# One convolved piece made a step earlier, and its successor's load issued a step earlier, in the RG-LRU recurrence of a hybrid mixer layer

## What is computed

```python
xc = dwconv(vx, conv_w, conv_b, 2, 1)          # latent; cc likewise of the context
for d, rev in enumerate((False, True)):        # forward and backward
    a_c, b_c = lru_coeffs(cc, ...)             # r, i = sigmoid(xc @ wa), sigmoid(xc @ wx) per head of 64
    h_c = linear_scan(a_c, b_c, None, rev)     # h_t = a_t h_prev + b_t
    h0 = h_c[:, 0] if rev else h_c[:, -1]
    a_x, b_x = lru_coeffs(xc, ...)             # a = exp(-8 r softplus(-lam)); b = sqrt(1 - a^2) * (i * xc)
    y_x = y_x + linear_scan(a_x, b_x, h0, rev)
```

## Time and profile before

| | us |
|---|---|
| median of 3 runs (lowest, highest) | 797.6 (796.71, 797.98) |
| the profiled execution, in all | 795.27 |
| its span | 793.2 |
| TensorE busy | 740.0 (93%) |
| VectorE busy | 534.0 (67%) |
| ScalarE busy | 449.4 (57%) |
| GpSimd busy | 273.5 (34%) |

### The profile page before, as it was taken

The page is one execution under the profiler, slowest core; times in us unless marked ns, Lnnn a source line. Parts: engine busy times, 40 slices in busy tenths (PEclk is TensorE's granted clock), DMA queues, the critical chain, the costliest instruction groups (busy, mean ns, idle before and its releaser), DMA issues.

```text
span 793.2 us, 9934 instructions
## 1 busy us (share of the span) xinstructions
PE 740.0 (93%) x3468; PEld 602.5 (76%) x3468; DVE 534.0 (67%) x811; ACT 449.4 (57%) x743; POOL 273.5 (34%) x321
## 2 busy tenths in 40 slices
PE   3876989999999998999998999989999999999997
PEld 1575767888888877888887887758787888888885
DVE  4377654759997789788996655776645665766532
ACT  4266652798786975887984982334535133534311
POOL 0022335243435254224433456223211145443421
PEclk9596999999999998999999999989999999999999
DMA  9998003334355245344453134344458667967531
GB/s 363 347 324 242 27 28 107 93 97 117 116 181 173 64 157 173 99 126 137 163 167 112 58 104 142 98 146 147 115 197 305 224 209 252 307 214 264 180 114 76
DMA packets 89218, 130.11 MB, mean 164 GB/s; under 512 B 22768, under 2 KB 54128, under 8 KB 87632
## 3 DMA queue, kind: packets, MB, share of 16 engines
q1 hardware_dynamic: 84800, 115.44, 45.0%
q0 software_dynamic: 4368, 14.03, 6.4%
HBM read 91.17 MB, written 38.27 MB: 163 GB/s over the span
## 4 chain that ended last, share of the span: by engine, by line
PE 72%; DVE 8%; issue 6%; DMA 5%; ACT 5%; POOL 3%; SPq 1%; DVEq 0%; ACTq 0%; POOLq 0%
PE bank L1543 23%; PE bank L1545 23%; PE bank L1544 23%; DMA wm<-in_w_mod 3%; DVE xg L1186 1%; ACT bank L878 1%; ACT fbuf L895 1%; POOL xTh L609 1%; DVE xTl L1194 1%; DMA pv<-scratch_u 1%; PE bank L1579 1%; DVE xg L1166 1%; DMA wraw<-in_w_in 1%; PE bank L1669 1%; PE bank L1559 0%
## 5 line engine op out<-in xcount | busy, mean ns | idle before, releaser
L1543 PE MATMUL bank<-xTh,wh 128*128 128x512 f32 (+1 forms) x592 | 237.0, 400 | 7.4 <-DVE xTl L1194 4.0
L1545 PE MATMUL bank<-xTh,wl 128*128 128x512 f32 (+1 forms) x592 | 231.3, 391 | 0.0
L1544 PE MATMUL bank<-xTl,wh 128*128 128x512 f32 x576 | 226.9, 394 | 0.0
L1543 PEld LDWEIGHTS bank<-xTh,wh 128*128 128x128 f32 x592 | 112.8, 190 | 32.9 <-DVE xTl L1194 5.7
L1545 PEld LDWEIGHTS bank<-xTh,wl 128*128 128x128 f32 x592 | 112.5, 190 | 23.5
L1544 PEld LDWEIGHTS bank<-xTl,wh 128*128 128x128 f32 x576 | 109.8, 191 | 22.5 <-issue 1.2
L1543 PE MATMUL bank<-xTh 128*128 128x512 f32 (+1 forms) x272 | 104.2, 383 | 1.9 <-issue 1.4
L1544 PE MATMUL bank<-xTl,xTh 128*128 128x512 f32 x256 | 99.6, 389 | 0.0
L1545 PE MATMUL bank<-xTh,xTl 128*128 128x512 f32 x256 | 99.6, 389 | 0.0
L911 ACT ACTIVATE ustage<-bank 128x512 f32<-128x512 f32 x56 | 33.0, 593 | 92.3 <-PE bank L1545 75.9
L609 POOL TENSOR_SCALAR sph<-xc 128x512 fp32r<-128x512 f32 (+1 forms) x36 | 26.9, 762 | 122.1 <-PE bank L1545 67.5
(11 more groups left out here) (192 smaller groups left out, 1428.8 us busy)
## 6 DMA issues: line engine op xcount, KB each, us to landing
scratch_u<-ustage SPq DMA_DIRECT2D x72, 256.0 KB, 3.2
wraw<-in_w_in SPq DMA_DIRECT2D x18, 512.0 KB, 5.2
wm<-in_w_mod SPq DMA_DIRECT2D x8, 1024.0 KB, 14.4
xg<-in_x SPq DMA_DIRECT2D x16, 512.0 KB, 9.2
yb<-scratch_y SPq DMA_DIRECT2D x32, 256.0 KB, 3.6
gb<-scratch_u SPq DMA_DIRECT2D x32, 256.0 KB, 5.0
xres<-in_x SPq DMA_DIRECT2D x16, 512.0 KB, 4.7
out<-tout SPq DMA_DIRECT2D x15, 512.0 KB, 3.0
```

The source lines that it names most:

```text
L1543: mm(out, wh_, xh_, start=first, stop=False)
L1544: mm(out, wh_, xl_, start=False, stop=False)
L1545: return mm(out, wl_, xh_, start=False, stop=last)
```

## The change

On GpSimd, `load_v(after + 2)` is issued in step s = NCH - 1 = 3 (the fourth step of a tile) instead of in the last one, s = 4. On VectorE, `conv(after + 1)` leaves the head of the last step, where it stood behind `gate_w_lo(t + 1)`, and stands at the end of the fourth step, behind its scans, its weight parts and its `gate_sum`, if it has one. Both happen for t = 0, 1 and 2.

```diff
@@ GpSimd's loop
                 if s == 2 and more:
                     load_gate_w(t + 1)
                     load_v(after + 1)
-                if s == NCH and more:
+                if s == NCH - 1 and more:
                     load_v(after + 2)
                 gated_input(q)
@@ VectorE's loop
                 if s == NCH and t + 1 < N_LRU:
                     gate_w_lo(t + 1)
-                    conv(after + 1)
                 for j in convs_in_step(q, 4):
                     conv_glu(j)
                 one_minus_a2(q)
...
                 if s == 2 and t + 1 < N_LRU:
                     conv(after)
+                if s == NCH - 1 and t + 1 < N_LRU:
+                    conv(after + 1)
                 if s == NCH and t + 1 < N_LRU:
                     conv(after + 2)
```

## The result

The changed kernel is faster: 790.66 us (median, 786.94 to 793.11) against 796.61 us (792.53 to 797.98) for the kernel before, measured beside it, a ratio of 0.9925 with a 95% interval of 0.9908 to 0.9943. That is 6.0 us, where 2.8 were forecast. The time lies 0.5 us under the low end of the range. Of the 4.1 us between 794.8 and 790.66, 1.0 is the kernel before itself, which the prediction took at 797.6; the rest is the saving. Faster was right in sign; the sum was less than half of what came.

The account below looks back on a forecast made before the run. TensorE was taken to bound the kernel, with step 9's stall a wait for VectorE's cvzl. Stall 1.8 plus clock 0.95, about 2.8 us saved, other terms 0, gave 794.8 us; range 791.2 to 797.4.

Parts of the forecast that it names:

- R1: Rival, step 9: whole stall goes, as cvz gets in ahead of Ib or holds are rarer; saves 6.4, 791.2 us; chance 0.13.
- the sign for "right": Step 9: TensorE's idle time before the conv unit would be 2 to 3 us if the forecast held.
- The kept part from Qb to the restart: Step 9: from Qb's start to TensorE's restart it takes 3.18 us, unchanged by the edit.
- the size of the stall: Step 9: moving the conv shrinks TensorE's stall by 1.8 us, from 4.33 to about 2.5.
- one gwh of 0.42 slips between: Step 9: a GpSimd gwh of 0.42 us delays VectorE's moved conv, which then ends at 291.4.
- the clock: Behind step 9's stall: 2.27 us of slow clock, saved in four executions of ten, counted as 0.9 to 1.0 us.
- edit 2: Moving load_v(after + 2) to the fourth step: worth 0 in step 8, -0.4 to +0.1, and 0 in the third tile's turn.
- The first tile's turn has nothing to give: Steps 3 and 4, about 180 to 215 us: no gain, since TensorE was busy throughout 137 to 280 us.
- The stall at 424.65, with its clock, stays: Step 16, second step of the fourth tile: TensorE's 3.16 us wait remains, since the change edits nothing there.
- TensorE didn't wait there: Step 14, third tile's turn: exchanging gwl and conv is worth 0, plus or minus 0.3 us.
- R3: Rival, steps 8 and 9: the moved load holds Ib, gates(9) start 1.7 us late; slower, about 799.3 us; chance 0.09.
- R2: Rival, step 9: conv stretches, Ib holds gwl and cvz, clock falls anyway; saves 0 to 1, about 797.1 us; chance 0.17.

Follow-up runs that it names:

- e6: Changed kernel with GpSimd's two Ib products of step 9 cut from 512 columns to 16, a probe only; ratio to the kernel before 0.9897.
- e8: Changed kernel with the last step's gwl moved behind cvzl, and cvzl ahead of wl in every step; ratio to the kernel before 0.9905.
- e4: Changed kernel with three more gwl instructions ahead of cvz in step 9, writing the same values; ratio to the kernel before 0.9941.
- e1: Changed kernel with the load back in the last step, so only the conv is moved; ratio to the kernel before 0.9967.
- e9: Changed kernel with both moves undone for the first tile (t=0) alone; ratio to the kernel before 0.9920.
- e5: Changed kernel with the load of the third tile's turn (t=2) back in its last step; ratio to the kernel before 0.9929.
- e3: Changed kernel with both moves kept for the second tile (t=1) alone, old places for t=0 and t=2; ratio to the kernel before 0.9957.
- e0: The changed kernel run and profiled again with no edit; ratio to the kernel before 0.9919.

## Why the prediction was off, point by point

**Right: what bounds the kernel, and where.** The two waits named "issue" were waits for VectorE's cvzl; e6 and e8 took the first away by touching only VectorE's and GpSimd's work, and every microsecond of idle time removed or put in (2.76 by the change, 1.24 by e4) came back in gates(9) to gates(10).

**Right in kind: cvz stands behind Ib.** Ib held the two pieces for 2.84 us, as the working said (2.6), and e6 shows the cause. R1's first mechanism, cvz in ahead of Ib, did not occur, though the saving came out near R1's 6.4. That the holds were fewer than the working assumed is R1's other half, and 1.57 us with the clock at 1.00 lies between the sign for "right" (2 to 3 us) and the one for R1 (under 1 us). The kept part from Qb to the restart was forecast at 3.18 us and is 298.50 - 295.32 = 3.18.

**Wrong, first step: the size of the stall, 2.5 forecast, 1.57 measured.** Counted from gates(9), the restart was due at 18.2 us and came at 17.28. The first error is in "one gwh of 0.42 slips between": nothing slipped in, the three instructions took 2.36 us, and they ended at 10.24 instead of 10.7. gwl ended at 11.3 instead of 12.0, Ib started at 11.0 instead of 11.7, cvz ended at 14.2 instead of 15.1. I took every meeting of VectorE and GpSimd as a hold of full length. In the 0.94 us between 18.22 and 17.28, the conv has 0.48, gwl 0.23 and cvz 0.23.

**Wrong, second step: the clock, 0.95 forecast, 2.18 measured.** I multiplied 2.27 us by a chance of four in ten, though the clock doesn't fall by a part: the fall is there or not. With 2.5 us of idle time the chance was about fair (it fell at 2.28, 2.51, 2.79, 2.81 and everything over 3; it held at 2.57, 2.65 and 2.66), but 1.57 is clear of it: it held in all five profiles with 1.54 to 1.58 us. So the first error fed the second, and 0.9 us became 2.2. The likeliest case should have been either 1.8 or 4.1 in all, and the range should have reached further down.

**Wrong, third step: edit 2 at zero.** "Which only brings Ib nearer to VectorE's gwl and cvz" is true, and the effect has the opposite sign: Ib ahead of cvz by 0.34 us holds the pieces for 1.41 and 1.51, Ib behind it by 0.37 (e1) holds the first for 3.20, and the second comes behind that. Together with the clock the load's 0.6 us of issue is worth 2.15 us in step 9. I had left it "in the sum" without asking what the sum was without it, and had it at zero for the first and the third tile, where e9 and e5 show the same long hold (2.87 and 3.25 us).

**Wrong, fourth step: the other tiles at zero.** "The first tile's turn has nothing to give" rested on TensorE's full busy time up to 280 us. But a window with all its time busy can still hide a wait shorter than a matmul: gates(5) started 0.15 us late behind spl in the kernel before, with no idle time listed. About 0.5 us up to gates(9) hangs on the first tile (e9, e3). "The stall at 424.65, with its clock, stays" holds for the profile after (3.14, 0.76), but not for e0, e4, e6 and e9, where it was 2.57 to 2.79, with the clock held in three of the four. "TensorE didn't wait there" was true of step 14 and missed the point: VectorE has no idle time from there to step 16, so what step 14 loses is waited for in step 16 (e5). The sentence that the prediction falls if steps 13 to 16 change by over half a microsecond was the right alarm, and e0, e3 and e5 ring it, with 25.57, 28.89 and 29.53 us from gates(16) to gates(17) where before it was 27.63.

**R3 did not occur.** The load at the fourth step waited for conv(10), as described, and Ib started at 277.24 right behind it. But gate_sum, free of Ib, shortened to 0.63 + 2.68 us from 1.31 + 3.60, and gates(9) came 0.5 us earlier instead of 1.7 later. The shorter gate_sum isn't what gained the half microsecond: with this load moved and the first tile's left in place (e3, e9) gates(9) came 0.3 us later than before. R2 did not occur either.

**The sum again.** Forecast 2.75 us; 0.96 more from the stall, 1.23 from the clock, 0.51 from the first tile and 0.03 from step 16 make the 5.48 of the profiled pair. The rest up to 6.0 lies within the spread between executions, in which step 16 alone moved by 2.03 us (e0).

## What to carry to other kernels

Where an idle time costs both its length and the clock behind it, work out on which side of the fall the changed idle time lands, and put the whole price or none of it into the likeliest case. Of a moved instruction, ask what the one behind it now meets: half a microsecond of DMA issue decided which of two engines went first, and with it 2.2 us. And once the stalled unit's path is written down (here cvz, cvzh, cvzl), put everything that isn't on it behind it; that gave as much again as the change (0.9847 against 0.9925).

## What the runs showed of the hardware

**Who waits.** A cvz piece, with two SBUF inputs, lasted 1.41 us when it began during Ib's first product, and 3.20 us when it began 0.37 us ahead of it (e1); before, an instruction begun 0.11 us ahead lasted 3.21. Both long ones end behind both products. In all twelve profiles the last steps of the first three tiles show the same: in the 10 with a DMA issue right ahead of Ib, one VectorE instruction begun during the issue lasted 2.86 to 3.36 us and ended behind both products; in the 26 without, none was held by more than 1.1 us. It isn't the issue alone, though: in step 8 of the kernel after, an spl begun at 277.91, within Ib's first product, lasted 2.45 us and ended behind both as well. Qb, with one input from PSUM, isn't held: it took 0.67 to 0.69 us beside Ib as away from it. The Trainium skill (SBUF — State Buffer, "Who interferes with whom") says that a VectorE instruction with two SBUF inputs and a GpSimd instruction that reads SBUF contend for an exclusive lock, and that the order of issue decides which of them blocks. The 1.41 us agree, since Ib had started first; 3.20 and 3.21 don't, where VectorE's had started first by the rows, and the measurement decides. In e5 the held gacc, 0.35 us long when undisturbed, could even have ended 0.2 us before Ib began. Why a short wait becomes two products long is open.

**The clock.** Measured by the distance between the gates, less the gap, the same code lost 1.4 to 2.7 us behind a fall to 1.2 GHz, and idle times between 2.3 and 2.8 us ended either way: at 2.51 it fell and at 2.66 it held.

**What stays open.** Why VectorE reaches step 14 up to half a microsecond earlier or later in different executions, from which the spread of step 16's idle time comes. How the first tile's load acts on gates(9). And the tail, 321.7 to 325.2 us: there the landing of DMAs differs between executions. From the chain that ended last, in order of time (start, us to landing), of the kernel after:

```profile
480.31 5.03 DMA scratch_y<-yrow
...
487.49 4.78 DMA pcwr<-in_conf_pw
```

and of the kernel before:

```profile
484.76 2.98 DMA scratch_y<-yrow
...
489.89 2.94 DMA pcwr<-in_conf_pw
```

The same two transfers, at the end of the recurrence, took 3.9 us longer in all. On TensorE's timeline of the kernel after this ends in a wait for the pointwise weights:

```profile
497.58 0.80 PE L1544 MATMUL bank<-pdh,pwh 128*128 128x512 f32 x1 [4.64 <-DVE pcwl L1402]
```

It was 1.23 us before. What makes these transfers slower in one execution than in another wasn't tried.
